# Moving the modulation sums of the second block into the first block's feed-forwards, and the loads of the inputs to SyncE

## The reference

```python
cond_lat, cond_ctx = jax.nn.silu(c), jax.nn.silu(c_ctx)      # 1024 values each
for i in range(DEPTH):                                       # DEPTH = 2
    mod  = (cond_lat @ ada_w[i] + ada_b[i])[:, None, :]      # ada_w[i]: 1024 x 6144
    modc = (cond_ctx @ ada_w[i] + ada_b[i])[None, None, :]
    sh1, sc1, g1, sh2, sc2, g2 = jnp.split(mod, 6, axis=-1)
    ...
    h = modulate(rmsnorm_2(x, norm1_g[i]), sh1, sc1)         # t * (1 + scale) + shift
```

## Time and profile before

| | |
|---|---|
| median of 3 runs | 5288.98 us (5283.82 to 5292.26) |
| profiled execution, its own time | 5287.55 us |
| its span in the trace | 5286.1 us |
| TensorE (PE) busy | 4641.8 us, 88% of the span |
| PE weight loads (PEld) | 3547.5 us, 67% |
| DVE busy | 2000.8 us, 38% |
| ACT busy | 1506.6 us, 29% |
| POOL busy | 564.9 us, 11% |
| mean DMA traffic | 67 GB/s |

### The profile page before, as it was taken

How to read it: one execution, slowest core, us unless ns; L and a number is a source line. 1 busy time by engine, 2 the same in 40 slices (tenths; PEclk the granted TensorE clock), 3 DMA queues, 4 the chain that set the end, 5 groups by cost and what they waited for, 6 DMA issues and landing times. The chain is left out here.

```text
span 5286.1 us, 77063 instructions
## 1 busy us (share of the span) xinstructions
PE 4641.8 (88%) x33686; PEld 3547.5 (67%) x33686; DVE 2000.8 (38%) x3024; ACT 1506.6 (29%) x2634; POOL 564.9 (11%) x419
## 2 busy tenths in 40 slices
PE   6798897899977996979899888888889999779999
PEld 4684793677756874947687626465678885447787
DVE  3534433355245335333454312336422130234323
ACT  2523231333334232322333312135221120213322
POOL 1213200001012024000010000101000000023000
PEclk9898897899978997979899888799899999879999
DMA  3031002222221220012122151000011114300222
GB/s 131 33 109 51 3 15 78 71 84 92 92 81 40 96 84 6 4 54 91 64 96 90 66 191 52 24 32 1 28 48 62 63 60 149 114 17 29 80 96 84
DMA packets 95888, 351.77 MB, mean 67 GB/s; under 512 B 9920, under 2 KB 11328, under 8 KB 94400
## 3 DMA queue, kind: packets, MB, share of 16 engines
q1 hardware_dynamic: 85824, 312.51, 17.9%
q10 hardware_dynamic: 9728, 34.32, 1.7%
HBM read 332.11 MB, written 14.68 MB: 66 GB/s over the span
## 5 line engine op out<-in xcount | busy, mean ns | idle before, releaser
L286 DVE TENSOR_TENSOR wlo<-ring,whi 128x1024 fp32r<-128x1024 f32 x494 | 606.8, 1229 | 1978.2 <-ACT whi L276 1974.6
L276 ACT CAST whi<-ring 128x1024 fp32r<-128x1024 f32 x494 | 518.6, 1050 | 2373.8 <-PE ps L326 2192.2
L323 PE MATMUL ps<-h_hi,whi 128*128 128x512 f32 x1552 | 621.8, 401 | 76.7 <-DVE h_lo L478 33.4
L326 PE MATMUL ps<-h_hi,wlo 128*128 128x512 f32 x1552 | 611.6, 394 | 0.0
L324 PE MATMUL ps<-h_lo,whi 128*128 128x512 f32 x1552 | 610.2, 393 | 0.0
L323 PE MATMUL ps<-hm_hi,whi 128*128 128x512 f32 (+1 forms) x1408 | 507.9, 361 | 52.5 <-POOL spread L1778 42.7
L324 PE MATMUL ps<-hm_lo,whi 128*128 128x512 f32 (+1 forms) x1408 | 479.9, 356 | 0.0
L326 PE MATMUL ps<-hm_hi,wlo 128*128 128x512 f32 (+1 forms) x1408 | 420.6, 356 | 0.0
L323 PEld LDWEIGHTS ps<-h_hi,whi 128*128 128x128 f32 x1552 | 295.7, 191 | 148.2 <-issue 42.8
L323 PEld LDWEIGHTS ps<-hm_hi,whi 128*128 128x128 f32 x1408 | 268.0, 190 | 134.1 <-POOL spread L1778 43.1
L323 PE MATMUL ps<-ac_hi,whi 128*128 128x512 f32 x880 | 329.1, 374 | 26.6 <-DVE ac_lo L478 24.8
(11 more groups left out here) (358 smaller groups left out, 7619.6 us busy)
## 6 DMA issues: line engine op xcount, KB each, us to landing
ring<-in_w SPq DMA_DIRECT2D x596, 512.0 KB, 3.3
x_spill<-x ACTq DMA_DIRECT2D x2, 2048.0 KB, 7.4
h_spill<-h ACTq DMA_DIRECT2D x2, 2048.0 KB, 7.9
m_spill<-m ACTq DMA_DIRECT2D x2, 2048.0 KB, 8.6
h<-h_spill ACTq DMA_DIRECT2D x2, 2048.0 KB, 8.1
ma<-m_spill ACTq DMA_DIRECT2D x2, 2048.0 KB, 8.1
x<-x_spill ACTq DMA_DIRECT2D x2, 2048.0 KB, 13.0
x<-in_x ACTq DMA_DIRECT2D x1, 2048.0 KB, 15.7
```

What stands on the lines that cost most here:

```text
L276: self.A.copy(self.hi[k % 2][:], raw).then_inc(self.s_cut_hi.h, 1)
L286: self.V.tensor_tensor(self.lo[k % 2][:], raw, self.hi[k % 2][:].bitcast(F32), ALU.subtract).then_inc(self.s_cut_lo.h, 1)
L323: T.matmul(ps[:, b, 0:cw], hi, xh(q, c0, cw), start=q == 0, stop=False, skip_group_check=True)
L326: m = T.matmul(ps[:, b, 0:cw], lo, xh(q, c0, cw), start=False, stop=q == kt - 1, skip_group_check=True)
```

## The change

1. The stream of weights is reordered. The 48 raw pieces of each modulation leave the head of the second block's layers. In each hybrid layer's feed-forward two raw pieces now follow every two cut pieces of the up projection (22 times), and two more pairs stand inside the down projection.
2. `modulation_sums(layer)` is new. It makes the sums of the second block's layer 0 in hybrid layer 0's feed-forward, and those of layer 1 in hybrid layer 1's. The condition is now 32 columns wide (2 filled, 30 of zeros), and four matmuls go to four column groups (32 columns of the array, 32 partitions of the bank each), so that one bank holds 4 x 512 outputs. After every second output column of the up projection PE issues such a group of four (22 times), and twice more in the down projection: 24 groups of four in a layer, 96 matmuls as before. Three times in a layer ACT copies a whole bank out (128x512), four matmuls with 8 columns turn it back, and DVE copies the result to `mod_sums`.
3. `modulation` keeps only its two fences and five small DVE operations.
4. The silu of the condition, and the two sines, are issued by ACT behind the first norm of layer 0 (`tables`). DVE makes both angle tables before that norm, on two buffers, without waiting for ACT.
5. Constants, positions and x are loaded by SyncE ahead of the first weights; the condition and the context behind the first 4 pieces. All engines wait for constants and positions only; ACT and DVE wait for x in `hybrid`.

In the diff, `pe_tick(n)` stands behind output column n of the up projection on PE's queue, the lines with `mod_act` at the head of ACT's step n, those with `mod_dve` at the end of DVE's.

```diff
-HYBRID = [(80, "cut"), ..., (64, "cut"), (16 * FT, "cut"), (8 * FT, "cut"), (80, "cut")]
-DIFF = [(384, "raw"), (128, "cut"), ...]
-GQA = [(384, "raw"), (80, "cut"), ...]
+HYBRID = [(80, "cut"), ...,
+          (64, "cut"), *[(16, "cut"), (16, "raw")] * FT, *[(24, "cut"), (16, "raw")] * 2, (128, "cut"), (80, "cut")]
+DIFF = [(128, "cut"), ...]
+GQA = [(80, "cut"), ...]
...
         for p in range(len(self.kinds)):
             slot = p % SLOTS
+            if p == SLOTS:
+                self.nc.sync.dma_start(self.cond[:], self.a["cond"]).then_inc(self.s_late.h, 16)
+                self.nc.sync.dma_start(self.X[:, :, S:T2], self.a["ctx"]).then_inc(self.s_late.h, 16)
...
+        A.wait_ge(self.s_ld_x.h, self.s_ld_x.n)
+        V.wait_ge(self.s_ld_x.h, self.s_ld_x.n)
         A.dma_start(self.x_spill.ap(), self.X[:, :, 0:S]).then_inc(self.s_st_x.h, 16)
...
         b_lo = self.norm_to(h, SEG1, lambda j, si: self.p1("pre", j), [7], TMP, h_hi, h_lo)
+        if layer == 0:
+            self.tables()
...
+    def modulation_sums(self, layer):
+        T, V, A, ps = self.T, self.V, self.A, self.ps
+        row = [self.view(f"mrow{i}", 42000 + 512 * i, 512) for i in range(2)]
+        steps = self.plan_raw(24 * 4, 4)
+        b_row, b_back, b_mods = self.s_mrow.take(3), self.s_mback.take(3), self.s_mods.take(3)
+
+        def pe(i):
+            a, k = divmod(i, DT)
+            if i == 0:
+                T.wait_ge(self.s_cond.h, 1)
+            if k == 0 and a == 2:
+                T.wait_ge(self.s_mrow.h, b_row + 1)
+            for g in range(4):
+                T.matmul(ps[32 * g:32 * g + 32, 4 + a % 2, :], self.cond[:, k, :], self.raw_of(steps[4 * i + g]),
+                         start=k == 0, stop=k == DT - 1, skip_group_check=True).then_inc(self.s_raw.h, 1)
+
+        def pe_back(a):
+            T.wait_ge(self.s_mrow.h, b_row + a + 1)
+            if a > 0:
+                T.wait_ge(self.s_mods.h, b_mods + a)
+            for q in range(4):
+                m = T.matmul(ps[:, 6, 8 * q:8 * q + 8], row[a % 2][:, q * P:(q + 1) * P], self.c("rows8", 8), start=True,
+                             stop=True, skip_group_check=True)
+            m.then_inc(self.s_mback.h, 1)
+
+        def act(a):
+            A.wait_ge(self.s_raw.h, steps[4 * (DT * a + DT - 1) + 3].value)
+            if a == 2:
+                A.wait_ge(self.s_mback.h, b_back + 1)
+            A.copy(row[a % 2][:], ps[:, 4 + a % 2, :]).then_inc(self.s_mrow.h, 1)
+
+        def dve(a):
+            V.wait_ge(self.s_mback.h, b_back + a + 1)
+            out = self.mod_sums[:, layer, 16 * a:16 * a + 16, :].rearrange("p (g q) c -> p q g c", q=4)
+            V.tensor_copy(out, ps[:, 6, 0:32].rearrange("p (q g c) -> p q g c", q=4, g=4)).then_inc(self.s_mods.h, 1)
+        return pe, pe_back, act, dve
...
+        def pe_tick(n):
+            if n % 2:
+                mod_pe(n // 2)
+            if n in (18, 34):
+                mod_back(n // 16 - 1)
...
+            if n in (16, 32):
+                mod_act(n // 16 - 1)
...
+            if n in (20, 36):
+                mod_dve(n // 16 - 1)
...
+        def down_pe_tick(n):
+            if n < 2:
+                mod_pe(2 * FT // 2 + n)
+            if n == 3:
+                mod_back(2)
...
     def modulation(self, layer):
         self.fence()
...
+        b = self.p2("ada_b", 48 * layer, 48).unsqueeze(2).to_broadcast([P, 48, 2])
+        self.vq(V.tensor_tensor(self.mods, self.mod_sums[:, layer, :, :], b, ALU.add))
...
     def start(self):
-        A.dma_start(con[:], self.a["con"]).then_inc(self.s_load.h, 16)
-        A.dma_start(tab[:].bitcast(I32)[:, 0, :], self.a["pos"]).then_inc(self.s_load.h, 16)
-        A.dma_start(self.X[:, :, 0:S], self.a["x"]).then_inc(self.s_load.h, 16)
-        A.dma_start(self.X[:, :, S:T2], self.a["ctx"]).then_inc(self.s_load.h, 16)
+        sync.dma_start(con[:], self.a["con"]).then_inc(self.s_load.h, 16)
+        sync.dma_start(tab[:].bitcast(I32)[:, 0, :], self.a["pos"]).then_inc(self.s_load.h, 16)
+        sync.dma_start(self.X[:, :, 0:S], self.a["x"]).then_inc(self.s_ld_x.h, 16)
...
+    def tables(self):
+        A = self.A
+        A.wait_ge(self.s_rest.h, 1)
+        A.activation(self.tab[:, 1, :], self.rest[0], ACT.Sin)
+        A.activation(self.tab[:, 0, :], self.rest[1], ACT.Sin).then_inc(self.s_sin.h, 1)
+        A.wait_ge(self.s_late.h, 32)
+        A.activation(self.cond[:], self.cond[:], ACT.Silu).then_inc(self.s_cond.h, 1)
```

More of the change, by code:

```diff
@@ L175, in __init__ @@
                     self.piece_of.append(p)
-        self.tile = 0
+        self.raw_pieces = [p for p, kind in enumerate(self.kinds) if kind == "raw"]
+        self.cut_tile = self.raw_tile = 0
         self.cut_end = {}
@@ L591, in hybrid @@
         self.mix_and_project()
-        self.conv_ffn()
+        self.conv_ffn(layer)
         self.layer_embedding(layer)
@@ L1677, in modulation @@
     def modulation(self, layer):
-        T, V, A, ps = self.T, self.V, self.A, self.ps
+        V = self.V
         self.fence()
-        row = [self.view(f"mrow{i}", TB2 + 512 * i, 512)[0:2, :] for i in range(2)]
-        condv = self.cond.rearrange("p (q c) -> p q c", c=2)
-        steps = self.plan_raw(12 * DT, 4)
-        b_row, b_back = self.s_mrow.take(12), self.s_mback.take(12)
-        def pe_back(n):
-            T.wait_ge(self.s_mrow.h, b_row + n + 1)
-            for q in range(4):
-                m = T.matmul(ps[:, 6, 8 * n + 2 * q:8 * n + 2 * q + 2], row[n % 2][:, q * P:(q + 1) * P],
-                             self.c("ident")[0:2, 0:2], start=True, stop=True, skip_group_check=True)
-            m.then_inc(self.s_mback.h, 1)
@@ L1726, in modulation @@
-        go(pe(), act(), dve())
+        b = self.p2("ada_b", 48 * layer, 48).unsqueeze(2).to_broadcast([P, 48, 2])
+        self.vq(V.tensor_tensor(self.mods, self.mod_sums[:, layer, :, :], b, ALU.add))
+        self.vdone()
+        for which, norm in ((0, "norm1"), (1, "norm2")):
+            g = self.p2(norm, 8 * layer, 8).unsqueeze(2).to_broadcast([P, 8, 2])
+            sc = self.mods[:, 24 * which + 8:24 * which + 16, :]
+            o = self.gs[:, 16 * which:16 * which + 16].rearrange("p (j c) -> p j c", c=2)
+            self.vq(V.tensor_scalar(o, sc, 1.0, None, ALU.add))
+            self.vdone()
+            self.vq(V.tensor_tensor(o, o, g, ALU.mult))
@@ L2309, in start @@
             self.vdone()
[L2310 to L2313 removed]
+            self.vq(V.tensor_scalar(r_, r_, 3.14159, -3.14159, ALU.min, ALU.max))
+            self.vdone()
+        self.rest = rest
+        V.drain().then_inc(self.s_rest.h, 1)
+    def tables(self):
[5 more added lines that the diff above has]
+        A.activation(self.cond[:], self.cond[:], ACT.Silu).then_inc(self.s_cond.h, 1)
+        self.s_cond.take(1)
     def whole(self):
@@ L2328, in whole @@
         G.wait_ge(self.s_par.h, e)
-        A.activation(self.cond, self.p2("cond", 0, 16), ACT.Silu).then_inc(self.s_cond.h, 1)
-        self.s_cond.take(1)
         self.diff_layer()
@@ L2334, in whole @@
         A.wait_ge(self.s_out.h, 16)
-        assert self.tile == PIECE * len(self.kinds)
+        assert self.cut_tile + self.raw_tile == PIECE * len(self.kinds)
         self.weights()
@@ L2425, in _constants @@
     put("eps", np.full((P, 1), EPS))
+    rows8 = np.zeros((P, 8))
+    for g in range(4):
+        for c in range(2):
+            rows8[32 * g + c, 2 * g + c] = 1
+    put("rows8", rows8)
     put("invf", np.tile(inv, 4)[:, None])
```

110 lines of the change are left out of this document (46 added, 64 removed).

## The result

The changed kernel takes 5202.89 us (median of 4 runs, 5194.77 to 5203.72) against 5290.19 us for the kernel before in the same job (4 runs, 5283.82 to 5292.26): ratio 0.9834, 95% interval 0.9816 to 0.9851. It is 87 us faster, not 143: 45 us above the end of the forecast's own range (5158) and 15 above that of the wider one (5188). Its profiled execution took 5203.1 us, with a span of 5201.6.

What follows compares the result with a forecast made beforehand. PE was taken as the bound, busy all the time in the up projection, with the modulations pure PE time. -192.5 (modulations) - 11.6 (start) + 60.7 (groups, turns) = -143.4 from 5287.55 gives 5144 us; own range 5130 to 5158, wider 5126 to 5188.

Steps and rivals of the forecast that it cites:

- D: Rival at the start: it gains nothing because context and ring pieces hold up the parameters and sines wait; 5156 us, chance 0.06.
- A: Rival in the groups: streamed data are the limit, each pass takes twice as long, 41 us more; 5185 us, chance 0.15.
- The modulations: Second block: both stretches of pure PE time vanish, saving 97.3 and 95.2 us, together 192.5.
- The groups: Hybrid feed-forwards: 48 groups of four matmuls, fully overlapped, add 1.13 us each, 54.2 us.
- the turns: Hybrid feed-forwards: turning rows back, three times a layer at 0.98 + 0.10 us, adds 6.5 us in all.
- Rival B: Groups in the feed-forwards do not overlap at all, 3.64 us each; 5265 us, chance 0.03.
- semaphore updates: Groups: by the skill's rule, 26.3 ns per concurrent update might add 3.8 us over 48 groups, giving 5148 us.
- The ring: Weight loads in the feed-forwards: some 170 GB/s, 3.8 us of cover left, so costed at nothing.
- Rival C: The weight ring starves in the feed-forwards, a pair needing 15.5 us instead of 12.1; 5300 us, chance 0.03.
- The start: Before the first product: norm 15.8 us earlier, less 4.2 us of ACT work, net 11.6 us; bounds 8 and 13.
- the landing of the parameters: At the start: parameters issued at 15.7 us share engines with the context, costing 0.5 us more; norm starts at 19.1.
- The 8.8 us: Start gain if the skill's drain of 1.38 us came with each table switch: two switches cost 5.3 us, not 2.6.

Runs made afterwards that it cites:

- e10: The changed kernel with 56 unused columns (224 bytes) behind the constants, putting moving operands at distance 0 modulo 512 from the weight halves; 5148.52 us, ratio 0.9742.
- e2: The kernel before with eight unused columns (32 bytes) at the end of its constants; 5343.16 us, ratio 1.0105.
- e11: e10 with layer 0's parameters loaded by SyncE ahead of x, angles made behind the norm, and the up projection's rounded activations at distance 0; 5134.68 us, ratio 0.9712.
- e9: e5 with all four matmuls of a group sent to one column group, sums of three quarters of the modulation left out; 5310.83 us, ratio 1.0043.
- e1: The changed kernel with activations 32 bytes further (distance 64 modulo 256 from the weight halves); 5157.11 us, ratio 0.9758.
- e5: The changed kernel with 24 unused columns behind the constants (distance 128 modulo 256); 5186.09 us, ratio 0.9809.
- e7: The kernel before with the new start alone, modulations in their old place; 5279.36 us, ratio 0.9981.
- e6: The kernel before with weight halves and activations moved together by 32 bytes; 5290.72 us, ratio 1.0005.
- e12: The kernel before with 256 bytes more at the end of its constants (distance 256); 5284.58 us, ratio 1.0.
- e3: The kernel before with sixteen unused columns (64 bytes) at the end of its constants; 5298.85 us, ratio 1.0019.

## Why the prediction was wrong, point by point

**The step that failed** is the one that was never costed. The sum -192.5 - 11.6 + 60.7 takes every matmul that the change leaves alone at its old pace, the 0.229 us of rows 1, and the text calls what lies outside the edits things that "stay as they are". The change's new buffers moved all moving operands by 1824 bytes against the stationary ones, and this costs 54.2 us: after against e10, by their spans, 5201.6 against 5147.4 (by the two ratios to before, 0.9834 and 0.9742, it is 49 us). In the kernel before, 32 unused bytes cost 58 us (e2). With the distance restored the kernel takes 5148.5 us, inside the forecast's own range of 5130 to 5158. No rival had this mechanism. D and A, at 5156 and 5185, were the nearest in time, and both are wrong as causes. The diff did show three allocations ahead of `big`; what it would mean could be guessed only from a difference that the trace of before held as well: its up projection, whose rounded activations are 128 bytes off, runs at 0.229 us a matmul, the last feed-forward at 0.226. Even that difference has the distance as only part of its cause: putting it right in e11 took 1.7 us from a feed-forward, some 1.6 ns for each of the up projection's 1056 matmuls, about half of the 3 ns.

**The modulations**, 97.3 and 95.2: right, by DVE's operations behind the fences. By stretch they gave 97.3 and 94.8.

**The groups**, 54.2 plus 6.5 for the turns: the overlap is right, and so is the sum, but three of its terms were off and cancelled. In e10, where nothing else in them differs, the two feed-forwards are 30.2 and 30.3 us longer, 60.5 in all against 60.7. The turns cost 0.89 each and not 1.08, 5.3 in all. The last group of each up projection costs nothing, since PE waits behind it at the fence anyway; the first product of the down projection in before:

```profile
1316.31 0.76 PE L323 MATMUL ps<-ac_hi,whi 128*128 128x512 f32 x1 [7.43 <-DVE ac_lo L478]
```

and in e10:

```profile
1331.22 0.77 PE L329 MATMUL ps<-ac_hi,whi 128*128 128x512 f32 x1 [6.43 <-DVE ac_lo L484]
```

The wait is shorter by the group's 1.00 us. So 46 groups cost (60.5 - 5.3) / 46 = 1.20 us each and not 1.13. Part of what the price left out stands in the timeline of the group further up: behind a group the step from L329 to L330 takes 0.34 us (1154.63 to 1154.97), not 0.23. Rival A (a limit on what is streamed at once) would have shown passes 0.86 apart; the eight take 1.00 us together. Rival B has its own measurement in e9: 3.55 us a group against its 3.64, and not what happens. Of the semaphore updates the prediction said, after the Trainium skill's "TensorE: Matmul & The Clock Gate", section "The cost: per-tile semaphore tail", that a group might hold up the next matmul by 3 x 26.3 ns. The traces do not show it: in e9, where passes and their updates come one by one, a group takes 3.55 us, 0.11 more than eight passes of 0.43; four at once, it takes 1.00, 0.14 more than two. The difference is 0.03 and not 0.08 us, and the long step behind the group is 0.34 us in e9 too (1107.94 to 1108.28). No run took the updates away.

**The ring** at no cost: right. PE busy for 200.00 of 200.00 us at 168 GB/s. Rival C falls.

**The start**, 11.6: too much by 3 us, and the term that failed is the landing of the parameters, 5.3 us instead of 2.7. They landed with the context, which had been issued 10 us earlier on another queue. In the traces of e1, e5, e7, e9 and e10, which have the same start, they took 4.3 to 5.2 us. That the traffic of that queue is what held them up is the likely reading; no run took the context away. The five ACT operations cost 4.1 us (44.45 to 48.52) where 4.2 was said. Between each table load and the function behind it lie 1.29 us; the drain of 1.38 us that the Trainium skill counts ("ScalarE: Activation LUTs", section "What ACT_TABLE_LOAD costs") does not show. The 8.8 us that this rule gave came close to the measured 8.7, for a reason that has nothing to do with it: a number that fits is not a cause that is shown.

Of the 4.8 us between 5144 and e10's profile (its span and 1.5 us around it), 2.8 are the start, read at the first product (50.84), and 2 the second modulation, whose stretch gave 93.2 us in e10 where 95.2 were forecast. The other stretches cancel: the first of hybrid 0 is 3 us shorter than its tables ask for (989.7 against 988.5 and 4.1), the rest are together 3 us longer. Stretches with waits vary by this much between kernels that should be equal there: the first of hybrid 0 took 988.5 us in before, 984.0 in e6 and 982.7 in e12.

## What to carry to other kernels

A new buffer is an edit to every operand allocated behind it. Where TensorE sets the time, print the byte distance between the stationary and the moving operand before and after (modulo 256 here), and compare the pace of an untouched stretch, matmuls in 100 us, before any other cause is sought. Work of an engine is worth moving to a place where that engine is busy all the time only if it gets cheaper there: here the groups of four made 192 us into 60, and by e9 it would have stayed 174 to 185 without them.

## What the runs showed of the hardware

- In these fp32r products (128x128 by 128x512, a new stationary operand for each) the pace at the full clock depends on the distance between the two operands' addresses in a partition: 226 ns at 0 and 256, 228 at 64, 231 at 128, 233 at 32. Moving both together changes nothing (e6). No other distance was measured by itself, and 256 stands for the period by two cases: 0 and 256 give 443 matmuls, 32 and 288 give 431 and 430. That reads of the two operands get in each other's way is the likely reading, since weight loads run beside the matmul before them; it is argued, not shown.
- The Trainium skill, "SBUF — State Buffer", section "SBUF: two separate sides", says that within the engine side only the port pair shared by VectorE and GpSimd causes contention. It speaks of engines against each other; inside TensorE the measurement finds a loss of 3% that depends on addresses alone.
- The rule is not the same for every shape. In the differential layer, with 768 columns in parts of 512 and 256, distance 64 was better than 0: 687.2 and 681.7 us in e3 for its attention and its feed-forward (with the second modulation) against 691.4 and 688.0 in before. Why is open. A kernel with a distance of its own for each layer was not tried.
- Four column groups with plain fp32 at the full clock overlap: eight passes of 512 columns take 1.00 us, two rounds of 0.43 and 0.14 besides, against 3.55 in one column group.
